# Attention of a two-layer decoder step: in the even steps the products with the values are issued behind the transposes and scores instead of ahead of them

## The reference, cut to what matters

```python
k_nope = jnp.einsum('bsc,chd->bshd', lat, w_uk)
v = jnp.einsum('bsc,chd->bshd', lat, w_uv)
# for each block of 128 queries
s = (jnp.einsum('bqhd,bkhd->bhqk', qn, k_nope)
     + jnp.einsum('bqhr,bkr->bhqk', qr, k_rope)).astype(jnp.float32) * SM_SCALE
s = jnp.where(k_pos[None, :] <= q_pos[:, None], s, -jnp.inf)
p = jax.nn.softmax(s, axis=-1).astype(v.dtype)
o = jnp.einsum('bhqk,bkhd->bqhd', p, v)
```

## Time and profile before

| | |
|---|---|
| runs of the kernel before | 1999.93, 2002.46, 2003.27 us; median 2002.46 us |
| the profiled execution | 2003.84 us, span 2002.0 us |
| mean granted clock of TensorE | 0.981 |
| TensorE matmuls | 1905.1 us busy, 95% of the span |
| TensorE weight loads | 1809.2 us, 90% |
| VectorE | 901.9 us, 45% |
| ScalarE | 560.6 us, 28% |
| GpSimdE | 738.9 us, 37% |

### The profile page before, as it was taken

The page is one execution under the profiler, slowest core; times in us unless marked ns, Lnnn a source line. Parts: engine busy times, 40 slices in busy tenths (PEclk is TensorE's granted clock), DMA queues, the critical chain, the costliest instruction groups (busy, mean ns, idle before and its releaser), DMA issues.

```text
span 2002.0 us, 31154 instructions
## 1 busy us (share of the span) xinstructions
PE 1905.1 (95%) x12391; PEld 1809.2 (90%) x12391; DVE 901.9 (45%) x1492; ACT 560.6 (28%) x997; POOL 738.9 (37%) x743
## 2 busy tenths in 40 slices
PE   6999999999998999999989999999999899999995
PEld 5998898898798999999989978998888899999994
DVE  5254666664173111536453546666624621133216
ACT  7123444443122100201251334444511311020002
POOL 3332443342235333444254333343313533334434
PEclk9899999999999999999999999999999899999997
DMA  6213221054712222232131141122474132223222
GB/s 229 61 43 128 76 66 62 30 176 157 260 36 72 69 68 58 88 88 69 30 130 54 44 171 52 37 68 62 166 251 143 33 94 64 68 69 91 69 64 85
DMA packets 94746, 183.96 MB, mean 92 GB/s; under 512 B 12086, under 2 KB 35942, under 8 KB 93964
## 3 DMA queue, kind: packets, MB, share of 16 engines
q1 hardware_dynamic: 73440, 135.43, 22.2%
q10 hardware_dynamic: 21180, 46.80, 6.2%
HBM read 150.19 MB, written 32.45 MB: 91 GB/s over the span
## 4 chain that ended last, share of the span: by engine, by line
PE 72%; DVE 13%; ACT 7%; issue 4%; POOL 1%; DMA 1%; ACTq 1%; DVEq 0%; SPq 0%; POOLq 0%; PEld 0%
PE PS L616 50%; PE PS L711 5%; PE PS L596 4%; PE PS L639 4%; DVE MX L1685 3%; DVE PTL L1673 2%; ACT PB L1258 2%; PE PS L696 2%; ACT PTH L1055 1%; PE PS L661 1%; PE PS L731 1%; DVE SUMA L1753 1%; POOL PB L534 1%; DMA RAW<-in_wstream 1%; PE PS L672 1%
## 5 line engine op out<-in xcount | busy, mean ns | idle before, releaser
L513 POOL CAST WH<-RAW 128x512 fp32r<-128x512 f32 (+3 forms) x292 | 205.4, 703 | 901.1 <-DMA RAW<-in_wstream 901.1
L515 POOL TENSOR_TENSOR WL<-RAW,WH 128x512 fp32r<-128x512 f32 (+3 forms) x292 | 382.0, 1308 | 23.5
L616 PE MATMUL PS<-XH,WH 128*128 128x344 f32 x1344 | 290.6, 325 | 10.3 <-ACT SGB L1300 9.6
L616 PE MATMUL PS<-XL,WH 128*128 128x344 f32 x1344 | 288.2, 323 | 0.0
L616 PE MATMUL PS<-XH,WL 128*128 128x344 f32 x1344 | 288.0, 323 | 0.0
L616 PEld LDWEIGHTS PS<-XH,WH 128*128 128x128 f32 x1344 | 228.5, 190 | 13.1 <-ACT SGB L1300 10.2
L616 PEld LDWEIGHTS PS<-XH,WL 128*128 128x128 f32 x1344 | 228.6, 191 | 0.0
L616 PEld LDWEIGHTS PS<-XL,WH 128*128 128x128 f32 x1344 | 227.7, 190 | 0.0
L534 POOL TENSOR_SCALAR PB<-PB,RC 128x128 f32<-128x128 f32 (+7 forms) x128 | 95.6, 747 | 308.0 <-DVE RC L1667 308.0
L1258 ACT ACTIVATE PB<-PS,NB 128x128 f32<-128x128 f32 (+7 forms) x128 | 94.8, 741 | 167.9 <-DVE NB L1686 167.6
L1842 DVE TENSOR_TENSOR SGP<-PS,SGP 128x1032 f32<-128x1032 f32 x16 | 19.7, 1233 | 239.8 <-PE PS L616 239.8
(11 more groups left out here) (277 smaller groups left out, 3860.1 us busy)
## 6 DMA issues: line engine op xcount, KB each, us to landing
RAW<-in_wstream SPq DMA_DIRECT2D x236, 256.0 KB, 2.7
PAGES<-in_pages SPq DMA_DIRECT2D x128, 320.0 KB, 4.9
spill_p<-PST ACTq DMA_DIRECT2D x16, 516.0 KB, 2.9
spill_g<-FST ACTq DMA_DIRECT2D x48, 172.0 KB, 1.9
SGL<-spill_g ACTq DMA_DIRECT2D x16, 516.0 KB, 4.5
PRJ<-spill_p ACTq DMA_DIRECT2D x16, 516.0 KB, 4.3
spill_v<-VSTG ACTq DMA_DIRECT2D x16, 512.0 KB, 2.8
VSP<-spill_v SPq DMA_DIRECT2D x8, 1024.0 KB, 5.3
```

The lines of the kernel that those rows point to most:

```text
L513: pool.tensor_copy(WH[:, slot, 0:size], RAW[:, slot, 0:size]).then_inc(w_high[slot], 1)
L515: pool.tensor_tensor(WL[:, slot, 0:size], RAW[:, slot, 0:size], f(WH[:, slot, 0:size]), ALU.subtract).then_inc(w_split[slot], 1)
L616: last = nc.tensor.matmul(PS[:, 3 * par + c, 0:CH], w[:, slot, at], x(k)[:, c * CH:(c + 1) * CH], start=(k == 0 and n == 0), stop=(k == kt ...
```

## The change

In the loop over the steps, `values` moves from the head of an even step to behind `scores`, still ahead of `fill`. Nothing else changes: the same instructions, with the same waits.

```diff
                     for n in range(16):
-                        if n >= 2 and n % 2 == 0:
-                            values(r, n // 2 - 1)
                         turn(r, n)
                         if n + 2 < 16:
                             scores(l, i, n + 2)
+                        if n >= 2 and n % 2 == 0:
+                            values(r, n // 2 - 1)
                         fill(l, i, n)
```

## The result

| | before | after |
|---|---|---|
| median of the runs | 2001.2 us (4 runs, 1996.59 to 2003.27) | 2024.36 us (4 runs, 2023.55 to 2027.42) |
| ratio to before | | 1.0117, 95% interval 1.0101 to 1.0132 |
| profiled execution, span | 2003.84, 2002.0 us | 2027.42, 2025.6 us |
| mean granted clock | 0.981 | 0.979 |

The changed kernel is 23.2 us slower. I had forecast 2019 us, 16.2 us slower than before, with a range of 2009 to 2026.

What follows compares the result with a forecast made beforehand. The prediction took the loop of ScalarE and VectorE, not TensorE, to set the round from step 10 on. 8 rounds x 2.03 us made 16.2 us, giving 2019 us, with a range of 2009 to 2026.

Steps and rivals of the forecast that it cites:

- TensorE is the bound: Rival: transposes and scores fill TensorE's waits ahead of values, 13.7 us go, 1989 us; chance 0.05.
- Transposes and scores earlier are worth nothing: Even steps: earlier transposes and scores counted at nothing where the loop of ScalarE and VectorE is the limit.
- The cost by steps: Lateness of the loop followed through the second round's even steps, reaching 2.03 us a round, 16.2 us over 8 rounds.
- the tail from the start of the fill to the copy: End of values in even steps: 0.16 us past the fill's start plus a 0.03 hop, 0.19 us in all.
- step 10: Fill 0.99 us later, high-part copy at 319.18 instead of 317.86, lateness 1.32 us.
- the walk: Step-by-step reckoning of lateness through the second round's timeline, from 0.79 us in step 2 to 2.03 at step 15.
- step 4: Transposes wait for the normalising, the three parts take 2.74 us, copy at 298.51 instead of 296.87: lateness 1.64 us.
- the upper bound: Round's lateness if neither step 2 nor step 8 gives anything back: 2.79 us, 22.3 us in all, 2025 us.
- Step 6, step 14: Step 6's short scores cost nothing; step 14 has no scores, values and transposes only change places; lateness stays.
- Step 8 gives back: Step 8: TensorE was the slower one, so lateness falls from 1.64 to 1.01 us at the exponential of block 10.
- nothing is given back: Same mechanism, with no lateness recovered in steps 2 and 8: 2025 us; chance 0.12.
- The end of the round: Step 15: TensorE's wait stays near 0.76 us, and the rest of the program is late by the loop's lateness.

Runs made afterwards that it cites:

- e4: Changed kernel, but the values products read XH and XL and ScalarE's wait for values goes (attention output wrong): 1999.72 us, ratio 0.9994 to the kernel before.
- e2: Against the kernel before, values moved behind the scores in steps 6, 8 and 14 only: 1998.17 us, ratio 0.9985.
- e1: Changed kernel, but every even step runs transposes, values, scores, fill: 2002.29 us against 2002.24 for the kernel before, ratio 1.0001.
- e7: Changed kernel, but in each layer's last pair GpSimdE's weight-slab split is parted, one piece going after block 10: 2021.07 us, ratio 1.0085 to the kernel before.
- e3: Against the kernel before, values moved behind the scores in steps 2, 4, 10 and 12 only: 2028.07 us, ratio 1.0116.
- e6: Against the kernel before, values moved behind the scores in steps 2 and 4 only: 2014.39 us, ratio 1.0060.
- e5: Against the kernel before, values moved behind the scores in step 12 only: 2007.35 us against 2002.21, ratio 1.0025.

## Why the prediction was right, point by point

**What bounds the kernel.** Right. The loop of ScalarE and VectorE sets the round. e4 shows it: TensorE's order is that of the changed kernel, only a wait of ScalarE is gone, and the time is back at that of before. The rival *TensorE is the bound*, which a reading by busy share supports, is out by sign and size for this change: after it TensorE is 95% busy as before, and the kernel is 23 us slower. Its 13.7 us were not there to be had by moving the transposes up: in e2 and e4 TensorE's waits in the second round fall only from 2.9 to 2.4 and 2.1 us, because the moved-up transposes then wait for the normalising, which follows the loop's exponential. e2 and e4 win 3 to 4 us in the rounds.

**Transposes and scores earlier are worth nothing.** Right where the loop is the limit (e1: +0.7 us in all rounds); in step 8, where TensorE was late, it is worth 0.5 us a round (e2).

**The cost by steps.** The size was too small: 2.03 us a round forecast, 22.4 / 8 = 2.8 measured. For the second round, lateness of the exponentials against before:

| exponential of block | forecast | measured |
|---|---|---|
| 4 | 0.68 | 0.77 |
| 6 | 1.64 | 1.79 |
| 10 | 1.01 | 1.25 |
| 12 | 1.32 | 1.83 |
| 14 | 2.03 | 2.63 |

Three terms make up most of the difference. First, the tail from the start of the fill to the copy. I took 0.19 us, with the hop of 0.03 us that follows transposes; after values it is 296.18 - 295.92 = 0.26, as 303.97 - 303.71 and 325.00 - 324.74 are. That is 0.07 us at each of five copies, 0.35 a round. Second, step 10. I let TensorE start its block when it was free; but the transposes, now first, must wait for the normalising of block 10, and start at 322.92 - 5.32 = 317.60 where the walk had 316.25 + 0.99 = 317.24. Part of this is lateness from before; of its own the step costs 1.83 - 1.25 = 0.58 where I had 0.31, and 0.07 of that is the tail again, so 0.20 is new. Third, the last pair of each layer, where this same exposure meets a split of 3.8 us on GpSimdE. I took the second round for all eight. The two rounds cost 3.6 us each, of which e7 takes away 1.2 each, 2.4 us in all.

The second round is not typical in step 4 either. There the normalising starts 0.51 us after the reciprocal has ended, in the seven other rounds 0.20, in both kernels; why is not known. This step costs 1.02 us in the second round (1.79 - 0.77) and 0.8 in the others. The walk, with 0.96, came near the 1.02 since it took its rows from that one round, and is too high here for the others.

So the mechanism was right and the size too small, 16.2 us against 23.2, and that the time still lies inside the range has some luck in it. The mean of 2.80 us a round is just above 2.79, the upper bound that I had worked out. I had said that I would be wrong if the rounds were not longer by 1 to 2.8 us: six are longer by 2.4 to 2.6, but the two last ones of a layer, 3.6 us, lie outside. No bound of mine had the split in it.

**Step 6, step 14.** Right: 40 waits are 5 a round, steps 2, 4, 8, 10 and 12. I had not listed step 8 among the copies that would wait for values, though the walk had it there.

**Step 8 gives back.** The size was about right (1.79 to 1.25, forecast 1.64 to 1.01), and the reason as I gave it, TensorE being the slower one, holds only with the values behind: e3 and e6 keep the whole delay. The bound *nothing is given back*, 2.79 us a round, came out close to the mean of 2.8, but not for its reason.

**The end of the round.** Right. The wait in step 15 grew from 0.76 to 0.90 us and did not swallow the delay. Within a layer the next round starts 19.75 us after the last exponential of this one, before the change 19.73 to 19.75. Outside the rounds the two profiles differ by 23.6 - 22.4 = 1.2 us: the stretch ahead of the first round is 2.7 us longer, that between the layers 1.6 shorter. No experiment here explains it. Between all the kernels profiled here, the first exponential starts between 211.5 and 216.1 us and the stretch between the layers takes 715.6 to 719.4.

**What I said would show it.** TensorE's new waits for normalising are in steps 6 and 14 and in step 4 of the second round alone; I had named 4, 12 and 14. Those of steps 7 and 15, and of step 10 in the last round of each layer (0.2 to 1.1 us), were there before and grew. In step 4 of the seven other rounds, in step 12 of all, and in steps 5 and 13, it is the low part of the block before (31 waits, 11.0 us) that comes last. In step 12 of the second round the walk had the wrong releaser, but at nearly the right time: normalising and low part end within 0.01 us of each other (328.66 + 0.80 and 328.78 + 0.69), and the transposes start at 329.62.

## What to carry to other kernels

When a product reads a buffer that another engine will overwrite, its end is a release, and everything put ahead of it in an in-order queue delays that release; look for who waits for the end of the moved work before looking at what the moved-up work could start. An engine that is 95% busy need not be the one that sets the pace: in a loop of two engines at 28% and 45% of the span, a delay of 0.8 us came out at the end of the round undiminished. Price a reordering step by step, with every round that differs: here four of the seven steps lost by the change, two (6 and 14) cost nothing, and one (8) gained.

## What was not expected of the hardware

A copy on ScalarE starts 0.03 us after the modelled end of the transposes that it waits for (312.15 + 0.30 to 312.48), but 0.09 us after the modelled end of the last values product (295.81 + 0.28 to 296.18). Ends of matmuls in the profile are modelled, and this case does not show which of the two is off.

The stretch ahead of the attention, whose code is the same in all kernels, differs between profiled executions by more than some of the effects here: the first exponential starts at 213.44 us in the kernel before and at 216.12 in the changed one, and at 211.53 in e2. Where the code is the same the rounds repeat to within 0.1 us (in e5, up to the exponential of block 12), which is why they were compared rather than the spans.
